# A three-mixer decoder layer in float32: VectorE in the scalar_tensor_tensor form, and GpSimd with all low weight halves

## The reference

```python
h = rmsnorm(x, norm1_g)
a1, a2, z, xbc, dt_raw, u, v = jnp.split(h @ w_in, [o1, o2, o3, o4, o5, o6], axis=-1)
ga = a1 * jax.nn.sigmoid(a2)
ca, new_hist_a = causal_dwconv(hist_a, ga, conf_conv_w, conf_conv_b)        # 31 taps
y_a = jax.nn.silu(layernorm(ca, conf_ln_g, conf_ln_b)) @ conf_w_out
xbc_c, new_hist_ssm = causal_dwconv(hist_ssm, xbc, ssm_conv_w, ssm_conv_b)  # 4 taps
...
y_ssd, new_h = ssd(xh, dt, a_neg, b_, c_, h_ssm)
y_b = rmsnorm(y_ssd * jax.nn.silu(z), ssm_norm_g) @ ssm_w_out
u = jax.nn.gelu(u)
vn = layernorm(jax.nn.gelu(v), gmlp_ln_g, gmlp_ln_b)
y_c = (u * chunk_spatial(vn, gmlp_w_s, gmlp_b_s)) @ gmlp_w_out
gates = jax.nn.sigmoid(h @ w_gate + b_gate).reshape(n, t, N_BRANCH, D_MODEL)
mixed = gates[:, :, 0] * y_a + gates[:, :, 1] * y_b + gates[:, :, 2] * y_c
x = x + mixed @ w_o
up = rmsnorm(x, norm2_g) @ ffn_w_up
...
x = x + (jax.nn.silu(agc) * av) @ ffn_w_down
```

## Time and profile before

| | before |
|---|---|
| median of three runs | 1029.4 us (1029.18 to 1032.2) |
| profiled execution, as a whole | 1031.2 us |
| its span, first to last instruction | 1029.4 us |
| TensorE busy | 1002.2 us (97%) |
| VectorE busy | 623.4 us (61%) |
| ScalarE busy | 381.2 us (37%) |
| GpSimd busy | 282.0 us (27%) |
| TensorE's mean granted clock | 0.988 |

### The profile page before, as it was taken

One profiled execution on the slowest core, in us unless ns is written; L12 is line 12 of the kernel. 1 busy time (PEld: TensorE's weight loads), 2 busy tenths in 40 slices (PEclk: granted clock), 3 DMA queues, 4 the chain that ended last, 5 costly groups with the idle time before them and its releaser, 6 DMA issues.

```text
span 1029.4 us, 19474 instructions
## 1 busy us (share of the span) xinstructions
PE 1002.2 (97%) x7994; PEld 980.2 (95%) x7994; DVE 623.4 (61%) x970; ACT 381.2 (37%) x544; POOL 282.0 (27%) x212
## 2 busy tenths in 40 slices
PE   5999999999999999999999999999999999999996
PEld 5999989989998999989999999999999999999996
DVE  4799879975547788796533335555540036666453
ACT  4322337653631665525222334433321122322210
POOL 3200000000030001452344334444434454444350
PEclk9999989999999999999999999999999999999997
DMA  7423227323322323415272222323223332321222
GB/s 237 147 83 99 65 62 63 66 63 92 89 73 62 104 83 117 171 41 185 82 248 85 83 86 80 93 92 99 64 62 93 100 110 89 99 66 53 76 59 87
DMA packets 42605, 97.96 MB, mean 95 GB/s; under 512 B 14640, under 2 KB 15536, under 8 KB 42544
## 3 DMA queue, kind: packets, MB, share of 16 engines
q1 hardware_dynamic: 42544, 97.10, 31.8%
HBM read 89.15 MB, written 7.93 MB: 94 GB/s over the span
## 4 chain that ended last, share of the span: by engine, by line
PE 86%; DVE 11%; issue 1%; POOL 1%; ACT 1%; DMA 0%; SPq 0%; DVEq 0%
PE accs L382 79%; DVE temps L1480 2%; DVE ca L1417 2%; DVE w_split L330 1%; PE misc L950 1%; PE misc L1112 1%; PE misc L956 1%; DVE part L444 1%; PE misc L1077 1%; PE misc L963 1%; PE misc L1128 1%; POOL w_split L330 1%; PE misc L1117 1%; PE misc L1096 1%; DVE xbc L2078 0%
## 5 line engine op out<-in xcount | busy, mean ns | idle before, releaser
L382 PE MATMUL accs<-h_split,w_split 128*128 128x272 f32 x4992 | 637.1, 289 | 4.6 <-POOL h_split L580 2.9
L382 PEld LDWEIGHTS accs<-h_split,w_split 128*128 128x128 f32 x4992 | 628.9, 189 | 10.2 <-issue 4.4
L330 POOL TENSOR_TENSOR w_split<-w_raw,w_split 128x1024 fp32r<-128x1024 f32 (+2 forms) x112 | 252.6, 2263 | 445.1 <-ACT w_split L325 422.3
L382 PE MATMUL accs<-branch,w_split 128*128 128x272 f32 x2208 | 284.8, 290 | 0.0
L382 PEld LDWEIGHTS accs<-branch,w_split 128*128 128x128 f32 x2208 | 280.2, 189 | 3.0 <-issue 2.8
L325 ACT ACTIVATE w_split<-w_raw 128x1024 fp32r<-128x1024 f32 (+3 forms) x168 | 160.0, 962 | 238.4 <-PE accs L382 238.2
L1417 DVE SCALAR_TENSOR_TENSOR ca<-part,params,ca 128x512 f32<-128x512 f32 x120 | 83.7, 749 | 0.4
L330 DVE TENSOR_TENSOR w_split<-w_raw,w_split 128x1024 fp32r<-128x1024 f32 (+1 forms) x56 | 62.1, 1109 | 29.0 <-ACT w_split L325 28.8
L2066 DVE TENSOR_TENSOR xbc<-accs,xbc 128x544 f32<-128x544 f32 x16 | 11.6, 725 | 95.6 <-PE accs L382 95.6
L2043 DVE TENSOR_TENSOR temps<-temps,mixed 128x512 f32<-128x512 f32 x22 | 40.7, 1850 | 26.5 <-ACT temps L920 26.5
L768 ACT ACTIVATE temps<-accs,params 128x544 f32<-128x544 f32 x24 | 17.2, 715 | 93.1 <-PE accs L382 93.1
(11 more groups left out here) (253 smaller groups left out, 710.8 us busy)
## 6 DMA issues: line engine op xcount, KB each, us to landing
w_raw<-in_ffn_w_up SPq DMA_DIRECT2D x44, 512.0 KB, 3.6
w_raw<-in_w_in_main SPq DMA_DIRECT2D x28, 512.0 KB, 3.6
w_raw<-in_w_gate SPq DMA_DIRECT2D x24, 512.0 KB, 3.7
w_raw<-in_ffn_w_down SPq DMA_DIRECT2D x16, 384.0 KB, 3.0
w_raw<-in_ffn_w_down SPq DMA_DIRECT2D x16, 320.0 KB, 2.9
xbc<-in_x SPq DMA_DIRECT2D x16, 272.0 KB, 5.7
w_raw<-in_w_in_z SPq DMA_DIRECT2D x8, 512.0 KB, 3.5
w_raw<-in_ssm_w_out SPq DMA_DIRECT2D x8, 512.0 KB, 3.6
```

The lines of the kernel that those rows point to most:

```text
L330: e.tensor_tensor(w_split[:, s, 1, 0:n], w_raw[:, s, 0:n], w_split[:, s, 0, 0:n].bitcast(F32), ALU.subtract).then_inc(w_lo[s], 1)
L382: mm = pe.matmul(accs[:, a, half, 0:HALF], w_split[:, s, wp, k * P:(k + 1) * P], rhs(s, k, xp, half), start=(first and k == 0 and n == 0), ...
```

## The change

Two things.

1. On VectorE, operations of the tensor_tensor form whose two operands both lie in SBUF are written as scalar_tensor_tensor with the factor 1.0: (a × 1.0) op b, which gives the same values. Operations that read PSUM keep their form, and so do `four_sum`'s. The decay of old states that GpSimd makes (`decayed`) stays tensor_tensor there. The taps and `x_conv` had the form already.
2. GpSimd makes all low weight halves. `lo`, `lo_ahead` and `order_next` go, with VectorE's 56 calls of `split_lo`. GpSimd makes them in the order of the phases, each behind its wait for the high half; nothing else on VectorE is moved.

The diff, cut to its core (the other operations are converted like these):

```diff
-            for s in range(SLOTS):
-                split_lo(pool, ph["G0"], 0, s)
+            splits(("VU", 1), *(("X", i) for i in range(3)))
+            splits(*(("G2", i) for i in range(4)))
+
+            splits(*(("G0", i) for i in range(4)), ("Z", 0))
...
+            def splits(*quads):
+
+                for name, i in quads:
+                    for s in range(SLOTS):
+                        split_lo(pool, ph[name], i, s)
+
+            splits(("A", 1), ("VU", 0))
             pool.wait_ge(acc_free[1], 4)
...
             for b in range(4):
-                lo_ahead("A", b // 2, 2 * (b % 2))
                 conf_taps(TAPS_A[0])
...
                 ready[0] = b + 1
-                lo_ahead("A", b // 2, 2 * (b % 2) + 1)
                 conf_taps(TAPS_A[1])
...
             for s in range(SLOTS):
-                lo_ahead("VU", 0, s)
                 conf_taps(TAPS_V)
...
-                link(dve.tensor_tensor(T(4), T(4), T(5), ALU.add))
+                link(dve.scalar_tensor_tensor(out=T(4), in0=T(4), scalar=1.0, in1=T(5), op0=ALU.mult, op1=ALU.add))
...
                         sil = T(2 + r, SEQ)
-                        dve.tensor_tensor(sil, sil, stat_n2[:, 0:SEQ], ALU.mult)
+                        dve.scalar_tensor_tensor(out=sil, in0=sil, scalar=1.0, in1=stat_n2[:, 0:SEQ],
+                                                 op0=ALU.mult, op1=ALU.mult)
```

More of the change, by code:

```diff
@@ L1370, in _ @@
                     dve.wait_ge(sem("n1_added"), j - 1)
-                dve.tensor_tensor(T(2), T(0) if j == 1 else T(2), T(j % 2), ALU.add).then_inc(sem("n1_added"), 1)
+                dve.scalar_tensor_tensor(out=T(2), in0=T(0) if j == 1 else T(2), scalar=1.0, in1=T(j % 2),
+                                         op0=ALU.mult, op1=ALU.add).then_inc(sem("n1_added"), 1)
             rstd("n1")
@@ L1746, in merge_second @@
                 dve.wait_ge(acc_free[1], p.pair0 + j + 1)
-                dve.tensor_tensor(mixed[:, j], mixed[:, j], T(j % 2), ALU.add).then_inc(sem("merged"), 1)
+                dve.scalar_tensor_tensor(out=mixed[:, j], in0=mixed[:, j], scalar=1.0, in1=T(j % 2),
+                                         op0=ALU.mult, op1=ALU.add).then_inc(sem("merged"), 1)
             def g0_slot(k):
@@ L1753, in g0_slot @@
                     merge_second(2 * i + s // 2)
-                lo(*(("G0", i + 1) if i + 1 < ph["G0"].quads else ("Z", 0)), s)
             for c in range(NCH):
@@ L1955, in merge_third @@
                 dve.wait_ge(sem("ns_stat"), 1)
-                link(dve.tensor_tensor(t, t, stat_ns, ALU.mult))
+                link(dve.scalar_tensor_tensor(out=t, in0=t, scalar=1.0, in1=stat_ns, op0=ALU.mult, op1=ALU.mult))
                 dve.wait_ge(acc_full[1], p.pair0 + j + 1)
@@ L1959, in merge_third @@
                 dve.wait_ge(acc_free[1], p.pair0 + j + 1)
-                dve.tensor_tensor(mixed[:, j], mixed[:, j], t, ALU.add).then_inc(sem("merged"), 1)
+                dve.scalar_tensor_tensor(out=mixed[:, j], in0=mixed[:, j], scalar=1.0, in1=t,
+                                         op0=ALU.mult, op1=ALU.add).then_inc(sem("merged"), 1)
             def new_states(n):
@@ L1969, in mixed_lo @@
                 dve.wait_ge(sem("mx_hi"), j + 1)
-                dve.tensor_tensor(branch[:, mixed_at(j)[1]], mixed[:, j], branch[:, mixed_at(j)[0]].bitcast(F32),
-                                  ALU.subtract).then_inc(sem("mx_lo"), 1)
+                dve.scalar_tensor_tensor(out=branch[:, mixed_at(j)[1]], in0=mixed[:, j], scalar=1.0,
+                                         in1=branch[:, mixed_at(j)[0]].bitcast(F32), op0=ALU.mult, op1=ALU.subtract).then_inc(sem("mx_lo"), 1)
             merge_third(0)
@@ L2001, in x2_lo @@
                     wait(dve, sem("n2_added"), j - 1)
-                    dve.tensor_tensor(T(5), T(5), T(2 + j % 2), ALU.add).then_inc(sem("n2_added"), 1)
+                    dve.scalar_tensor_tensor(out=T(5), in0=T(5), scalar=1.0, in1=T(2 + j % 2),
+                                             op0=ALU.mult, op1=ALU.add).then_inc(sem("n2_added"), 1)
             p = ph["WO"]
```

140 lines of the change are left out of this document (78 added, 62 removed).

## The result

| | before | with the change |
|---|---|---|
| median of the runs, us | 1029.29 (4 runs, 1028.59 to 1032.20) | 1047.35 (4 runs, 1044.50 to 1049.87) |
| profiled execution / its span, us | 1031.2 / 1029.4 | 1045.09 / 1043.3 |
| ratio, with its 95% interval | 1 | 1.0167 [1.0137, 1.0197] |

The kernel became slower by 18.1 us in the median and by 13.9 us from span to span. Two of its four runs lie near 1045 us (mean granted clock 0.983 to 0.985) and two near 1049.7 us (0.980); the trace is of a run of the first kind. The sum of the prediction was made on the span, so it is compared with the 13.9 us.

A forecast was written before the change was run, and what follows sets the result against it. TensorE was busy 1002.2 of 1029.4 us, with VectorE also full in stretches up to about 220 us, which decides. Terms 7.8 + 6 + 1 + 1 = 15.8 us on 1029.4 us gave 1045 us, range 1033 to 1062 us.

The forecast's parts named there:

- form: VectorE's tensor_tensor operations rewritten as scalar_tensor_tensor: no price taken, with +1 us as the bound.
- products of phase A: TensorE waits for VectorE's late products L1450 in phase A: 0.7, 2.2 and 1.8 us, together 4.6 us.
- behind at the channel sum: In phase VU, at the sum TensorE wants near 109 us, TensorE stands 9.6 us behind the kernel before.
- behind at the sum of squares: Near 128 us in the kernel before: its 1.8 us wait goes, leaving TensorE +7.8 us.
- phase X: VectorE's full stretch from 154.40 us to the mixed block at 208.73 us: +4.5 to +7 us, taken as +6 us.
- later: G2 and G0: VectorE's idle time covers everything in G2; +1 us for both, 0 to 3 as bounds.
- clock as a whole: Half-speed stretch from 130 us goes, new ones come at waits near 114 and 215 us: net +1 us, −2 to +4.
- The turn: A GpSimd split beside VectorE work on two SBUF operands costs VectorE 2.08 us, in either form; bounds 0 and 2.8 us.
- The first: Rival: VectorE's scalar_tensor_tensors pass GpSimd by, so 28 splits before 226 us are freed at no cost: 1022 us; chance 0.06.
- the second: Rival: turns mostly fall in VectorE's gaps, half the hits in A and VU vanish: 1031 to 1038 us; chance 0.13.
- the fourth: Rival: G0's heads slip 1 us at each of 8 pairs, up to four more half-speed stretches: 1052 to 1066 us; chance 0.12.
- the third: Rival: back-to-back taps keep GpSimd out, TensorE waits for late low halves in A, VU, X: 1050 us; chance 0.03.

The follow-up runs named there:

- after_memset: The changed kernel, but GpSimd fills the 28 low halves of the early phases by two memsets each instead of the subtraction: 1022.56 us, ratio 0.9922.
- copy_first: The changed kernel with ScalarE's copy of the turned samples moved ahead of its SiLU of block 7 in X: 1046.36 us, ratio 1.0158 to the kernel before.
- late_on_pool: The kernel before, with only the 28 late low-half splits (in G2, G0 and Z) moved to GpSimd: 1031.26 us, ratio 1.0004.
- x_on_pool: The kernel before, with only the 12 splits of X's quads 1 and 2 and G2's quad 0 moved to GpSimd: 1036.96 us, ratio 1.0068.
- splits_only: The kernel before, with all low halves made by GpSimd and every operation's form unchanged: 1045.58 us, ratio 1.0156.
- sums_first: The kernel before, with VectorE's sum of squares moved ahead of the convolution of the sample tokens at the head of X: 1025.60 us, ratio 0.9953.

## Why the prediction was right, point by point

The forecast was 1045 us. That the profiled execution took 1045.09 us is luck: the sum forecast +15.8 us on the span, and +13.9 us was measured there, while the median rose by 18.1 us to 1047.35 us, between the two kinds of runs. The mechanism held. Its terms did less well than their sum, as the starts of the same matmuls in the two traces show. "Clock" is what a half-speed stretch costs against the same matmuls in the other trace.

| term | forecast, us | measured, us |
|---|---|---|
| form | 0 (to +1) | 0: ratio 0.9998 |
| products of phase A | +0.7, +2.2, +1.8 | +1.4, +2.3, +0.1 |
| behind at the channel sum | 9.6 | 10.4 |
| behind at the sum of squares, without the clock | 7.8 | 8.6 |
| phase X, without the clock | +6 | +3.9 |
| later, without the clock | +1 | +0.2 |
| clock as a whole | +1 (−2 to +4) | +1.2: +2.3, −3.4, +3.8, −1.5 |
| span in all | +15.8 | +13.9 |

- **The turn.** 2.08 us for a split, whatever VectorE's form, was right. The tensor_scalar at 38.65 us lost 2.21 us, the sum at 115.68 us lost 2.01 us against the one behind it, and L2062 kept its 1.85 us. after_memset shows that GpSimd's read is the cause: without it the taps take 745 ns. The forecast of "over 1000 ns" for the tap's mean was a little too high: 963 ns.
- **Phase A.** The products start at 55.61, 69.87 and 81.95 us; the walk through the deadlines gave their ends as 56.0, 70.1 and 83.8 us. The first two end at 56.5 and 70.7 us and cost 3.7 us on TensorE where 2.9 us were forecast. The third ends at 82.8 us, 12.1 us after the second where the walk had 13.7: the split of 78.25 us was kept out (see below). 3.8 us in all for the 4.6.
- **Channel sum.** TensorE starts it at 119.24 us where it was 108.88 us: 10.4 us behind for the 9.6 of the walk, and the wait is 6.2 us long. A half-speed stretch of 6.8 us begins at 117.1 us, inside that wait, and so costs only 2.3 us. That at 130 us, which the kernel before has (3.4 us), is gone. With both, TensorE stands 7.5 us behind the kernel before after the sum of squares, and doesn't wait for it, as forecast.
- **Phase X.** This is the term that was mis-sized. VectorE starts the stretch of the earlier trace rows at 161.91 us for 154.40 us and its last operation at 220.17 us for 208.73 us, so it lost 3.9 us there and not 6. Two of the seven splits in it, at 176.2 and 193.3 us, were kept out (see below) and cost VectorE nothing and 0.8 us, where 2.08 us were taken for each. TensorE's waits are 4.8 and 1.3 us, 6.1 together, for 1.7 and 0.4 us before, so some 4 us of waiting are new. And the delay didn't come through the mixed block first but through the convolution, ScalarE's SiLU and its copy; copy_first showed that this detour adds nothing.
- **Clock.** Gone at 130 us and new at the two long waits were all forecast. The stretch near 210 us is 10.2 us long and begins 1.6 us before the wait ends: the matmuls from 210.80 us to 223.62 us took 9.0 us before and take 12.8 us now, 3.8 us more. The half-speed stretch of 3.4 us at 475 us, which the kernel before has, is missing after the change and gives 1.5 us back; nothing in the prediction looked there. That the clock as a whole came out near the +1 is partly luck, for this piece wasn't in it. Without the clock 12.7 us were measured where 14.8 were forecast: 0.8 us too little up to the sum of squares, 2.1 too much in X and 0.8 too much later.
- **Later.** G0 costs nothing; late_on_pool shows it for all 28 late splits. The bound of 0 was right, the +1 taken wasn't.'s window from 311 us is a shifted copy, but not all behind it: the clock at 475 us differs.
- **Rivals.** The first (1022 us) is excluded by the taps at 963 ns, the second (1031 to 1038 us) by the measured time and by VectorE's 70.2 busy of 70.8 us, the fourth (1052 us and more) by G0. Of the third, GpSimd kept out, the mechanism exists at a few splits, but TensorE waits for no low half: each was needed three slots later. The prediction's sentence that "a queue of VectorE work doesn't keep it out" was wrong as a general one.

The Trainium skill ("SBUF — State Buffer", section Who interferes with whom) says that such a lock is held for the full instruction. The prediction took its 2.08 us to speak against that. The two pairs of rows above don't: the tensor_scalar ends at 41.40 us, 0.3 us after the split beside it (41.11), and the sum at 118.42 us, 0.6 us after its split (117.83). VectorE's operation so ended only behind the split's end. It loses less than the split's 2.4 us, as only 0.3 of its own 0.54 us, and 0.6 of 0.73 us, come after that end. For a sum of prices the measured loss of 2.0 to 2.2 us is the one to use: the walk with 2.08 us came out within 0.7 us at both sums of VU.

## What to carry to other kernels

Before work goes from a full VectorE to GpSimd, look for one place in the trace where GpSimd's form already runs beside VectorE's: the longest of the neighbours gives the price of the turn, and if it is more than what VectorE is rid of, the move loses exactly where it was wanted and is free only where it isn't needed. Another form of the same two-tensor operation on VectorE doesn't change the turn; a GpSimd operation that reads nothing avoids it. And a wait of TensorE can be worth more than its length: 1.8 us of waiting cost 5.1 us in the kernel before (3.3 us in x_on_pool), and one moved line of VectorE's order gave that back.

## What the runs showed of the hardware that I had not expected

- **GpSimd can be kept out.** The split of 78.25 us could start while VectorE ran eight taps, and took 6.04 us instead of 2.38 us. VectorE's timeline over the same time, after:

```profile
76.65 5.38 DVE L1418 SCALAR_TENSOR_TENSOR ca<-part,params,ca 128x512 f32<-128x512 f32 x8
```

  Eight taps in 5.38 us: none of them lost a turn. The split ended at 84.29 us, 2.34 us after VectorE had gone over to the products (81.95 us), which read PSUM, and that is about the time of a split that runs alone. It happened to few: in the same trace one at 130.3 us took 3.60 us, and two at 176.2 and 193.3 us took 4.79 and 8.53 us; one of splits_only at 150.3 us took 9.16 us. Beside other taps GpSimd got its turn at once, at 96.82 us (2.71 us) for instance. These taps follow one another without waiting; the four decays of the earlier trace rows, where the turns alternate, may differ in that. No run tests it, so what decides stays open.
- **One SBUF input is enough to be held up.** The tensor_scalar L1415, with one tensor from SBUF, took 2.75 us at 38.65 and 2.61 us at 90.90 us beside GpSimd's splits, and 0.54 us before. The prediction counted only operations with two.
- **The same wait can have another price in clock.** The half-speed stretch was 6.8 us behind the wait of 1.8 us for the sum of squares in the kernel before, and 3.4 us behind the same wait in x_on_pool. Behind the wait of 1.7 us for the mixed block there was none before and one of 3.4 us in sums_first. At waits of 6.2 and 4.8 us it was 6.8 and 10.2 us long, but began inside them, and what fell in the wait cost nothing. The length of a wait alone doesn't give its price in clock, and one trace doesn't either.
- **GpSimd's memset is free for VectorE.** 52 memsets of 1024 columns in the full stretches left the taps at 745 ns.
